# The tail of a routed encoder layer: the sum that the last scatter leaves alone is reloaded ahead of it

## What is computed

```python
x = layer_norm(DEEPNORM_ALPHA * x + mix, ln1_g[l], ln1_b[l])      # x1 below
ffn = moe(x, ...)          # 64 experts, top 8 of each token, and 1 shared expert
x = layer_norm(DEEPNORM_ALPHA * x + ffn, ln2_g[l], ln2_b[l])      # the output

def expert_block(acc, blk):            # blocks of 128 tokens of one expert
    tok, g, e = blk
    xb = x_pad[tok]
    h = jax.nn.silu(xb @ w_gate[e]) * (xb @ w_up[e])
    y = (h @ w_down[e]) * g[:, None].astype(xb.dtype)
    return acc.at[tok].add(y), None
```

## Time and profile before

| | us |
|---|---|
| median of 3 runs | 1469.63 |
| lowest and highest run | 1464.76, 1471.03 |
| the profiled execution | 1470.6 |
| its span in the trace | 1469.0 |
| TensorE busy (matmul records) | 1326.4 (90% of the span) |
| DVE, ACT, POOL busy | 965.4, 798.5, 457.1 |

### The profile page before, as it was taken

One profiled execution on the slowest core, in us unless ns is written; L12 is line 12 of the kernel. 1 busy time (PEld: TensorE's weight loads), 2 busy tenths in 40 slices (PEclk: granted clock), 3 DMA queues, 4 the chain that ended last, 5 costly groups with the idle time before them and its releaser, 6 DMA issues.

```text
span 1469.0 us, 25653 instructions
## 1 busy us (share of the span) xinstructions
PE 1326.4 (90%) x6359; PEld 1098.0 (75%) x6360; DVE 965.4 (66%) x1121; ACT 798.5 (54%) x1057; POOL 457.1 (31%) x425
## 2 busy tenths in 40 slices
PE   8967946699998599999999999999999999999955
PEld 6865636578886378888888888888888888878842
DVE  4599756457675269577577745556577579776736
ACT  4131255412222368677677746657677678767724
POOL 0000010124456133333334333333333343333321
PEclk9998977789998799999999999999999999999977
DMA  6112041113667769998899978887889899999646
GB/s 232 44 58 72 0 146 53 58 72 87 70 111 177 226 219 346 303 344 292 248 311 334 344 251 243 272 251 241 262 303 328 283 324 340 325 324 315 212 119 277
DMA packets 77889, 323.68 MB, mean 220 GB/s; under 512 B 22592, under 2 KB 24752, under 8 KB 52640
## 3 DMA queue, kind: packets, MB, share of 16 engines
q1 hardware_dynamic: 43152, 251.05, 48.7%
q0 software_dynamic: 33552, 68.04, 20.1%
q10 hardware_dynamic: 1152, 4.19, 0.8%
HBM read 290.46 MB, written 67.34 MB: 244 GB/s over the span
## 4 chain that ended last, share of the span: by engine, by line
PE 79%; DVE 10%; DMA 6%; issue 2%; ACT 2%; SPq 0%; POOL 0%; ACTq 0%; DVEq 0%; POOLq 0%
PE ps L1594 34%; PE ps L1612 18%; PE ps L1511 6%; PE ps L1397 6%; PE ps L1422 4%; DVE cv L994 4%; PE ps L1547 3%; DMA raw<-in_w_up 2%; PE ps L1536 2%; PE ps L1625 1%; DMA xb_d<-ysb 1%; PE ps L1469 1%; PE ps L1498 1%; DMA out<-acc 1%; DVE whl L908 1%
## 5 line engine op out<-in xcount | busy, mean ns | idle before, releaser
L1594 PE MATMUL ps<-wgu,xTe 128*128 x2304 | 550.8, 395 | 5.3 <-issue 4.1
L1594 PEld LDWEIGHTS ps<-wgu,xTe 128*128 128x128 f32 x2304 | 427.1, 189 | 93.3 <-issue 8.0
L1612 PE MATMUL ps<-wdn,hT 128*128 (+1 forms) x1236 | 301.3, 393 | 16.1 <-ACT ysb L789 15.9
L1264 DVE TENSOR_TENSOR wgu<-raw,wgu (+1 forms) x128 | 287.7, 2288 | 7.9 <-issue 3.4
L1612 PEld LDWEIGHTS ps<-wdn,hT 128*128 128x128 f32 x1236 | 233.9, 190 | 66.2 <-issue 17.5
L721 ACT CAST wgu<-raw (+1 forms) x128 | 246.7, 1928 | 2.7 <-SPq L411 2.7
L1269 DVE TENSOR_TENSOR xTe<-ps,xTe 128x512 fp32r<-128x512 f32 x194 | 124.6, 684 | 133.9 <-ACT xTe L784 133.9
L1264 DVE TENSOR_TENSOR wdn<-raw,wdn x64 | 146.7, 2293 | 60.2 <-ACT wdn L777 58.4
L789 ACT ACTIVATE ysb<-ps,idx 128x512 f32<-128x512 f32 x188 | 119.0, 684 | 122.5 <-PE ps L1612 122.5
L565 POOL DMA_INDIRECT xa_d<-ysb,idx x48 | 87.8, 1830 | 261.6 <-ACT ysb L789 202.1
L565 POOL DMA_INDIRECT xb_d<-ysb,idx x47 | 91.3, 1943 | 248.1 <-ACT ysb L789 231.7
(11 more groups left out here) (228 smaller groups left out, 1228.4 us busy)
## 6 DMA issues: line engine op xcount, KB each, us to landing
raw<-in_w_gate SPq DMA_DIRECT2D x64, 1024.0 KB
raw<-in_w_up SPq DMA_DIRECT2D x64, 1024.0 KB
raw<-in_w_down SPq DMA_DIRECT2D x64, 1024.0 KB
wraw<-in_w_in SPq DMA_DIRECT2D x10, 512.0 KB, 3.3
xin<-in_x SPq DMA_DIRECT2D x8, 512.0 KB, 8.2
wraw<-in_w_kv SPq DMA_DIRECT2D x8, 512.0 KB, 3.3
raw<-in_w_out SPq DMA_DIRECT2D x4, 1024.0 KB, 7.9
xres<-in_x SPq DMA_DIRECT2D x8, 512.0 KB
```

The source lines that it names most:

```text
L1264: V.tensor_tensor(dst, raw_, hi.bitcast(F), ALU.subtract).then_inc(done, 1)
L1594: last = mm(ps[:, 2 + s, :], xTe[:, s, st, d], wgu[:, w, mo, d].rearrange("p a n -> p (a n)"), start=(d == 0 and st == 0 and mo == 0), sto ...
L1612: last = mm(ps[:, 5 + h, :], hT[:, s, st, c], wdn[:, w, mo, c, h * 512:(h + 1) * 512].rearrange("p a n -> p (a n)"), start=(c == 0 and st ...
```

## The change

- **Order.** SP no longer waits for all scatters before it reloads anything. It reads `past` into a register, waits for all scatters of the sum that the last item doesn't add to, and loads that sum in two DMAs of 2 MB (`early`). The other (`late_`) is loaded in eight DMAs of 512 KB, one for each tile, after the last scatter has landed and the three compute engines have reported. Which sum is which depends on whether `past` is odd; the two are now halves of one tensor `sum_d`, addressed by a register.
- **Scatter.** `add_rows` scatters into `sums`, all 2048 rows. So a list entry has three words: the token, the token plus 1024, the gate.
- **Buffers.** `acc` has a buffer for each tile, and DVE's wait for a store's landing is gone.
- **Sums.** `ADDED` is (4, 6). DVE adds tile t + 2 ahead of its step t. TensorE adds the other six, in two parts: for the first four the early half as soon as the first 2 MB are in, the late half tile by tile.
- **End waits.** ACT, DVE and TensorE report to `s_endC` and wait for 3 of them; only POOL reports to `s_endR`, and only SP waits for it.

```diff
-ADDED = (0, 1, 2)
+ADDED = (4, 6)
...
-        tg = at("tg", 202, [128, NT, K, 2], U32)
+        tg = at("tg", 202, [128, NT, K, 3], U32)
...
-        xa = at("xa", 0, [128, NT, D])
-        xb = at("xb", 32, [128, NT, D])
-        acc = [at("acc0", 176, [128, D]), at("acc1", 180, [128, D]), at("acc2", 184, [128, D])]
+        early = at("early", 96, [128, NT, D])
+        late_ = at("late_", 0, [128, NT, D])
+        acc = at("acc", 32, [128, NT, D])
...
-        list_d = nc.dram_tensor("list_d", [LIST, 2], U32, kind="Internal").ap()
-        xb_d = nc.dram_tensor("xb_d", [S, D], F, kind="Internal").ap()
+        sum_d = nc.dram_tensor("sum_d", [2, S, D], F, kind="Internal").ap()
+        xa_d, xb_d = sum_d[0], sum_d[1]
+        sums = sum_d.rearrange("a t d -> (a t) d")
+        list_d = nc.dram_tensor("list_d", [LIST, 3], U32, kind="Internal").ap()
...
-            sp.wait_ge(s_endR, 4)
+            sp.wait_ge(s_tabs, 1)
+            past = sp.value_load(nit[0:1, 1:2], min_val=E, max_val=MAX_ITEMS - NT)
+            late = sp.value_load(nit[0:1, 2:3], min_val=E - 2, max_val=MAX_ITEMS - NT - 2)
+            sp.wait_ge(s_yd[0], 16 * (past // 2))
+            sp.wait_ge(s_yd[1], 16 * ((late + 1) // 2))
+            sp.sem_inc(s_seen, 1)
+
+            def rows_of(which, t0, n):
+                tiles = sum_d.rearrange("a (t p) d -> (a t) p d", p=128)
+                return tiles[bass.ds(which * NT + t0, n)].rearrange("t p d -> p t d")
+
+            for n in range(2):
+                sp.dma_start(early[:, 4 * n:4 * n + 4], rows_of(past % 2, 4 * n, 4)).then_inc(s_early[n], 16)
+            sp.wait_ge(s_endC, 3)
+            sp.wait_ge(s_endR, 1)
             for t in range(NT):
-                for tile, rows in ((xa, xa_d), (xb, xb_d)):
-                    sp.dma_start(tile[:, t], rows[t * 128:(t + 1) * 128, :]).then_inc(s_sums[t], 16)
+                sp.dma_start(late_[:, t:t + 1], rows_of((past + 1) % 2, t, 1)).then_inc(s_late[t], 16)
             for t in range(NT):
                 sp.wait_ge(s_o, t + 1)
-                sp.dma_start(out[t * 128:(t + 1) * 128, :], acc[t % 3][:]).then_inc(s_out[t % 3], 16)
+                sp.dma_start(out[t * 128:(t + 1) * 128, :], acc[:, t]).then_inc(s_out, 16)
...
             g.iota(tg[:, :, :, 0], pattern=[[128, NT], [0, K]], base=0, channel_multiplier=1).then_inc(s_pt2, 1)
+            g.iota(tg[:, :, :, 1], pattern=[[128, NT], [0, K]], base=S, channel_multiplier=1).then_inc(s_pt2, 1)
...
-            for n in range(7):
-                g.dma_start(list_d[S + n * 12288:S + (n + 1) * 12288, :].rearrange("(p j) a -> p (j a)", p=128),
-                            fillw[:]).then_inc(s_fill, 16)
+            for first in range(S, LIST, 8192):
+                n = min(8192, LIST - first)
+                g.dma_start(list_d[first:first + n, :].rearrange("(p j) a -> p (j a)", p=128),
+                            fillw[:, 0:n * 3 // 128]).then_inc(s_fill, 16)
...
                 g.indirect_dma_start(
-                    out=(xa_d, xb_d)[c % 2], out_offset=bass.IndirectOffsetOnAxis(ap=idx[:, c % RING, 0:1], axis=0),
+                    out=sums, out_offset=bass.IndirectOffsetOnAxis(ap=idx[:, c % RING, c % 2:c % 2 + 1], axis=0),
                     in_=ysb[:, c % 2], in_offset=None, compute_op=ALU.add,
-                    bounds_check=S - 1, oob_is_err=False).then_inc(s_yd[c % 2], 16)
+                    bounds_check=2 * S - 1, oob_is_err=False).then_inc(s_yd[c % 2], 16)
...
-            act.wait_ge(s_endR, 4)
+            act.wait_ge(s_endC, 3)
...
             def normalise(t):
-                y, s = acc[t % 3][:], t % 2
+                y, s = acc[:, t], t % 2
                 if t == 0:
                     v.wait_ge(s_g2, 32)
-                if t >= 3:
-                    v.wait_ge(s_out[t % 3], 16 * (t // 3))
...
+            def add(t):
+                v.wait_ge(s_early[t // 4], 16)
+                v.wait_ge(s_late[t], 16)
+                step(V.tensor_tensor(acc[:, t], early[:, t], late_[:, t], ALU.add))
+                settle()
+                v.sem_inc(s_added, 1)
+
             for t in range(NT):
-                if t in ADDED:
-                    v.wait_ge(s_sums[t], 32)
-                    step(V.tensor_tensor(acc[t % 3][:], xa[:, t], xb[:, t], ALU.add))
-                    settle()
-                    v.sem_inc(s_added, 1)
+                if t + 2 in ADDED:
+                    add(t + 2)
                 if t == 0:
+                    v.wait_ge(s_pc, 1)
                     moments(t)
...
-            pe.wait_ge(s_endR, 4)
-            for t in range(NT):
-                if t in ADDED:
-                    continue
-                if t >= len(ADDED) + 4:
-                    pe.wait_ge(s_acc, t - 3)
-                pe.wait_ge(s_sums[t], 32)
-                for h in range(2):
-                    for rows in (xa, xb):
-                        last = mm(ps[:, 2 * (t % 4) + h, :], ident[:], rows[:, t, h * 512:(h + 1) * 512],
-                                  start=(rows is xa), stop=(rows is xb))
-                last.then_inc(s_pc, 1)
+            pe.wait_ge(s_endC, 3)
+            def add_part(t, rows):
+                for h in range(2):
+                    last = mm(ps[:, 2 * (t % 4) + h, :], ident[:], rows[:, t, h * 512:(h + 1) * 512],
+                              start=(rows is early), stop=(rows is late_))
+                return last
+
+            summed = [t for t in range(NT) if t not in ADDED]
+            for t in summed[:4]:
+                pe.wait_ge(s_early[t // 4], 16)
+                add_part(t, early)
+            for n, t in enumerate(summed):
+                if n >= 4:
+                    pe.wait_ge(s_acc, t - 3)
+                    pe.wait_ge(s_early[t // 4], 16)
+                    add_part(t, early)
+                pe.wait_ge(s_late[t], 16)
+                add_part(t, late_).then_inc(s_pc, 1)
```

More of the change, by code:

```diff
@@ L134, in build @@
         ysb = at("ysb", 176, [128, 2, D])
-        idx = at("idx", 201.9375, [128, RING, 2], U32)
+        idx = at("idx", 205.375, [128, RING, 3], U32)
         cmp_ = at("cmp_", 196, [128, 2, NE])
@@ L147, in build @@
         eps2 = at("eps2", 192.0625, [128, 1])
-        g2 = at("g2", 112, [128, D])
-        b2 = at("b2", 116, [128, D])
+        g2 = at("g2", 128, [128, D])
+        b2 = at("b2", 132, [128, D])
         epst = at("epst", 207.71875, [128, 1])
@@ L279, in build @@
         s_endR = sem("s_endR")
-        s_sums = [sem(f"s_sums{t}") for t in range(NT)]
+        s_early = [sem(f"s_early{n}") for n in range(2)]
+        s_late = [sem(f"s_late{t}") for t in range(NT)]
+        s_endC = sem("s_endC")
         s_g2 = sem("s_g2")
@@ L288, in build @@
         s_o = sem("s_o")
-        s_out = [sem(f"s_out{s}") for s in range(3)]
+        s_out = sem("s_out")
         W_JOBS = ["gate0", "a0", "gate1", "a1", "u0", "u1", "K0", "K1", "K2", "K3",
@@ L444, in _ @@
             sp.dma_start(b2[:], a["ln2_b"].to_broadcast([128, D])).then_inc(s_g2, 16)
-            sp.wait_ge(s_endR, 4)
+            sp.wait_ge(s_tabs, 1)
[11 more added lines that the diff above has]
+            sp.wait_ge(s_endR, 1)
             for t in range(NT):
-                for tile, rows in ((xa, xa_d), (xb, xb_d)):
-                    sp.dma_start(tile[:, t], rows[t * 128:(t + 1) * 128, :]).then_inc(s_sums[t], 16)
+                sp.dma_start(late_[:, t:t + 1], rows_of((past + 1) % 2, t, 1)).then_inc(s_late[t], 16)
             for t in range(NT):
                 sp.wait_ge(s_o, t + 1)
-                sp.dma_start(out[t * 128:(t + 1) * 128, :], acc[t % 3][:]).then_inc(s_out[t % 3], 16)
-            for s in range(3):
-                sp.wait_ge(s_out[s], 16 * len(range(s, NT, 3)))
+                sp.dma_start(out[t * 128:(t + 1) * 128, :], acc[:, t]).then_inc(s_out, 16)
+            sp.wait_ge(s_out, 16 * NT)
         @block.gpsimd
@@ L492, in _ @@
             g.memset(cumb[:], 0.0).then_inc(s_pt2, 1)
-            g.wait_ge(s_pt2, 7)
-            for n in range(7):
-                g.dma_start(list_d[S + n * 12288:S + (n + 1) * 12288, :].rearrange("(p j) a -> p (j a)", p=128),
-                            fillw[:]).then_inc(s_fill, 16)
+            g.wait_ge(s_pt2, 8)
+            for first in range(S, LIST, 8192):
+                n = min(8192, LIST - first)
+                g.dma_start(list_d[first:first + n, :].rearrange("(p j) a -> p (j a)", p=128),
+                            fillw[:, 0:n * 3 // 128]).then_inc(s_fill, 16)
             def rstd(n):
@@ L520, in _ @@
             mix_lo(1)
-            g.wait_ge(s_fill, 16 * 7)
+            g.wait_ge(s_fill, 16 * -(-(LIST - S) // 8192))
             for t in range(NT):
@@ L823, in step_act @@
                 act.wait_ge(s_dn, i - 1)
-                y_out(s, 1.0 / ALPHA if shared else idx[:, bass.ds((i - 2) % RING, 1), 1:2].bitcast(F).rearrange("p a n -> p (a n)"))
```

(29 more changed lines are left out.)

3 lines of the change are left out of this document (1 added, 2 removed).

## The result

The changed kernel takes 1461.81 us (median of 20 runs, 1457.11 to 1466.15), the kernel before, run beside it, 1469.91 (20 runs, 1464.76 to 1476.73). The ratio is 0.9943, 95% interval [0.9933, 0.9953], or 0.57% faster: 8.4 us by the ratio, 8.1 by the two medians. (From here on a gain in us is worked out from the ratio.) The prediction said 1465.6, 4.0 us faster, in a range of 1461.0 to 1470.5.

The account below looks back on a forecast made before the run. Mostly TensorE's expert matmuls, untouched; so the last 60 us were priced: tile 0 ready 1434.2 + DVE 27.2 + POOL wait 0.5 + store 3.1 = 1465.0 against 1469.0, hence 1469.63 - 4.0 = 1465.6 us. Range 1461 to 1470.5.

Parts of the forecast that it names:

- 1. The early load: Tail reload: two 2 MB loads issued at 1414.8 at best, done together with the last scatter at 1429.0.
- the rival in which SP sees the semaphore 3 us late: Tail, SP's wait for xb: late tile 0 later, time 1467.4; no own chance, the slow part of the forecast's 0.65.
- 2. The last scatter among loads: Last scatter beside the early load: lands at 1428.5, between 1424.3 and 1431.9; 4 us of the gain given back.
- The loop's row of up to 13.7 us: Expert loop, scatter beside weight loads: took up to 13.7 us, giving the last scatter's upper bound, 1431.9.
- an estimate of 1425.6: Last scatter's landing if queues alternate packet by packet, each of 8 rows an engine held up by one 4 KB read.
- 3. The late load: Tail, after the last scatter: issued at 1428.8, late tile 0 in at 1432.3, the next ones every 1.3 us.
- 4. TensorE: TensorE's adds in the tail: early half 8.5 us, done at 1430.1, hidden behind DMA; tile 0 ready at 1434.2.
- 5. DVE's chain: DVE in the tail from tile 0 on: 27.2 us of work plus 0.5 waiting for POOL's power; 7.9 us of holes go.
- 6. The last store: Final output store at the end of the tail: unchanged at 3.1 us.
- the fast rival: Tail: scatter and load do not hinder each other, scatter lands at 1424.3, time about 1461.5; chance 0.22.
- 7. The rest: Wider list entries, more fills, one tensor of twice the rows, renamed end waits, outside the tail's priced terms: all at 0.
- the loop before 1400 shifted by a microsecond or more: Expert loop ahead of the tail: a shift this large was named as a sign of a wrong forecast, excluded by 7. The rest.

Follow-up runs that it names:

- e3_buffers: The kernel before with an output buffer for each tile and nothing else: 1469.86 us against 1471.44, ratio 0.9993.
- e1_lists: The kernel before with three-word lists, both sums in one tensor and scatters into its 2048 rows, old tail: 1463.13 us against 1471.44, ratio 0.9945.
- e5_three: The kernel before with list entries of three words (12 bytes), keeping two tensors, old scatters and old tail: 1458.85 us against 1467.62, ratio 0.9941.
- e2_tail: The changed kernel with the old two-word lists, two tensors and a fixed choice between the sums: 1470.01 us against 1471.44, ratio 0.9982.
- e9_size: The kernel before with a larger list tensor and 11 fills, still 8-byte entries and lists 8192 bytes apart: ratio 1.0007 to the kernel before.

## Why the prediction came out as it did

The number fell into the range by luck. The tail, the only part that the sum priced, gave about half of the 4.0 us; the lists, priced at nothing, gave nearly all of the 8 that the whole kernel shows. The measured 0.57% lies where the prediction put a chance of 0.24 (faster by over 0.5%), and not within 0.5%, where it put 0.71. Part by part:

*1. The early load:* right. SP issued it 6.57 us after the second to last scatter (1400.43 to 1407.00); predicted were 1408.24 to 1414.8, 6.56. So the rival in which SP sees the semaphore 3 us late did not come about.

*2. The last scatter among loads:* right in kind, 10.96 us where 10.3 was taken. With the early load held back it is 6.14. The loop's row of up to 13.7 us was the useful witness. The Trainium skill's rule (DMA: Bandwidth & Descriptors, section Queues, rings and completion order), read as one load's packet for each of the scatter's rows, made an estimate of 1425.6 - 1418.17 = 7.4 us; the measurement decides against that reading. It took one 4 KB read as the packet, while that section gives 9 to 17 descriptors as typical of one; how many a packet had here no run shows.

*3. The late load:* right. Landing 1421.31, tile 0 used from 1425.16, 3.85 us; predicted 3.8.

*4. TensorE:* nearly. The early half took 9.3 us (8.5 predicted), since the clock stayed at 0.50 for its first 4 us, until about 1419, and was back at 1.00 from 1420. It was through at 1424.42, before late tile 0; the late half took 2.1 to the first statistics (1.9). In all DVE began 16.9 us after the scatter's issue instead of 16.0.

*5. DVE's chain:* too short. 1427.25 to 1456.25 are 29.0 us, predicted 27.2 + 0.5. The holes are small: four of 0.43 to 0.45 us at L1374, each released by POOL's power, 1.8 us in all where 0.5 was taken. That power takes 1.3 to 1.6 us for just these four tiles (1434.68 and 1447.65 are two of them) and 0.54 to 0.57 for the other four; why is open. ACT's 2.9 us a tile plus this is more than DVE's 2.64, and the two adds gave less slack than I had counted.

*6. The last store:* right, 3.05 us.

These add up: 0.9 us at the front and 1.3 in the chain, so 4.0 became 1.8 to 2.0. The output buffers, to which part 5 gives 5.8 us of DVE's holes, were worth about 1 by themselves (`e3_buffers`). DVE's chain is 7.5 us shorter in the changed kernel (29.0 for 36.5) also because half of TensorE's adds are done ahead of it; this is read from the two traces, no run takes it alone. (In the fast rival the ends should read 1460.4 to 1461.2, 0.1 more; nothing hangs on it.)

*7. The rest:* **this is the step that failed.** "I put all of this at 0": the fills and the scatters were counted as instructions on POOL, whose queue hides them, and that part holds. What was not priced was the effect of the lists' writes on other queues. The row that could have warned was in the trace before: SP's queue needs 5.7 us of engines for a MB from 342 to 475, while reloads ran at 410 GB/s, 2.4 us for a MB. The forecast lists "the loop before 1400 shifted by a microsecond or more" as a sign that part 7 is wrong, and that is what happened. What the runs showed in place of the 0: with the new lists and the old tail the kernel is 8.1 us faster (`e1_lists`), with the new entry alone 8.7 us (`e5_three`). Of the rivals, none had this cause: the fast one foresaw a scatter unhindered by loads, which is shown wrong.

## What to carry to other kernels

Price a change of layout on every queue that moves data at the same time, not only on the queue that issues it: compare the engines' busy time for a MB in that stretch with a clean one. Count the gain of a removed wait only up to the next limit behind it (5.8 us of waiting were worth about 1). When a tail must be reloaded, order the transfers by the time at which each tile is used, and keep large loads away from a small transfer that others wait for.

## What was unexpected of the hardware

With scatters of 128 entries, 8 bytes each, into 64 lists that start 8192 bytes apart, SP's transfers took 5.7 us of all engines for a MB in the kernel before (6.2 in `e2_tail`, 4.7 in `e9_size`); in the other layouts they took 2.9 to 4.1, while the small writes themselves showed 1.1 to 1.4% of the engines in all of them. The slowest of the eight stores of 512 KB then landed after 16.1 to 18.1 us (four profiles); with any other layout after 7.6 to 11.6 (ten profiles). Changing 8192 to 8448 with the same entries brought 52.9% down to 33.9% of the stretch. The Trainium skill (DMA: Bandwidth & Descriptors, Specifications) states that transfers below 512 bytes are done by reading, modifying and writing. All widths tried here lie below that, so by this rule alone they would not differ; the runs do.
